# Two spellings of one filling transfer in a fused encoder layer

## The chip, the cores and the metric

The kernel runs on one core of one Trainium2 chip. The time is that of the device, in microseconds (us). The kernel before took 1100.84 us, the median of three runs (1099.44 to 1101.90).

## The reference

One layer of a streaming encoder is computed in float32 for 512 prompt rows and 64 sample rows of width 1024:

```python
h = rmsnorm(x, g_mix)
rq, rk, rv, rg, dq, dk, dv, gr, gd = project(h, w_in, pos, g_q, g_k)      # one 1024 x 8192 product
y_r = retention_out(o_r, rg, g_ret, w_ret_o)     # silu(rg) * rmsnorm(o_r), times w_ret_o
y_d = diff_out(o_d, g_sub, lam_init, w_diff_o)   # differential attention, times w_diff_o
x = x + (sigmoid(gr) * y_r + sigmoid(gd) * y_d) @ w_out
x = x + hier_moe(rmsnorm(x, g_ffn), ...)         # top-1 of 4 groups, top-2 of its 4 experts, 16 experts, SwiGLU
```

For the experts each token's row is sent to one of 640 slots of each of its two experts. The kernel fills the first 128 slots of every expert beforehand with "empty" rows (zeros, and the number of a row that no one reads).

## The kernel before

Every product with a weight is made of three matrix products on TensorE (high and low parts; lines 449 to 451). Weights come from HBM in blocks of 1 MB, `dense_load(n)`, numbered n = 0 to 43. Blocks 0 to 31 are `w_in` (16 chunks of 512 columns, two blocks each), 32 to 35 `w_diff_o`, 36 to 39 `w_ret_o`, 40 to 43 `w_out`. The block's buffer is one of four (`raw`), so that block n is issued when block n-4 has been used up. ScalarE makes the high part (`dense_hi`, line 392) and VectorE the low part (`dense_lo`, line 397), for the two blocks of the next chunk while the present chunk is multiplied, at its tiles t = 1 and t = 2. A chunk has five tiles of rows (t = 0 to 3 of the prompt, 4 of the sample), and two PSUM banks take turns: the product of a tile starts when the tile before the last one has been read out.

The order is written out by hand for each engine, and each engine works through its own list in order. SyncE (SP in the profile) issues the weight loads and the fills of the slots. GpSimd (POOL) issues everything else: it stores the projections z (`z_gr` is the last section) into HBM and loads them again as gates. Gates `gd`, `rg`, `gr` are 1280 KB halves. Each is 320 packets of 4 KB. The two halves of `rg` are issued only once all stores of z have landed (line 630 is `load_gate`). The projected gate `gd` passes a sigmoid on ScalarE (`open_gate`, line 961).

After the last chunk of `w_in` follow six chunks that are called x = 0 to 5: x = 0 and 1 multiply the attention output by `w_diff_o` (blocks 32 to 35), x = 2 and 3 the retention output by `w_ret_o`, x = 4 and 5 the merged sum by `w_out`. In x = 0 VectorE has this list for each tile: read the product out into `od` (line 1412), normalise the retention output `ro` (line 1305) and multiply it by both halves of `rg` (line 1376). In x = 1, TensorE transposes the tiles of `ro` (line 1624), ScalarE and VectorE split them (`s_hi`, line 829; `s_lo`, line 1161).

The scratch tensor `x_slots` in HBM has rows of 1056 floats (4224 bytes), 640 for each of 16 experts, and 256 rows of padding. It is filled by four transfers, one behind each of blocks 32 to 35, each for four experts (line 521), by one for the padding (line 525) and one more that sets two tiles of `y` (line 526), both behind block 36. Nothing reads them before the tokens are sent out, from 735.6 us on.

Of the kernel before, what the change touches and what calls it, by code (L numbers as in the profile page):

```python
# [14 lines left out]
P = 128  # L15
# [16 lines left out]
NE, NG, EPG = 16, 4, 4  # L32
NR = NG + NE
CAP = TT * P
XW = D_MODEL + 32
# [77 lines left out]
def build(nc, a, o):  # L113
# [161 lines left out]
    def scratch(name, rows, cols):  # L275
        return nc.dram_tensor(name, (rows, cols), f32, kind="Internal").ap()
# [5 lines left out]
    x_slots = scratch("x_slots", PAD + 2 * P, XW)  # L282
# [7 lines left out]
    def sem(name):  # L290
        return nc.alloc_semaphore(name)
# [31 lines left out]
    y_init, slots_empty = sem("y_init"), sem("slots_empty")  # L323
# [12 lines left out]
    def chunk_block(n):  # L336

        c, half = divmod(n, BPC)
        if c < IN_CHUNKS:
            w, c0 = a["w_in"][0], SECTION[c][1]  # L340
        else:
            p, j = divmod(c - IN_CHUNKS, 2)
            w, c0 = a[("w_diff_o", "w_ret_o", "w_out")[p]][0], j * COLS
        return w[half * 512:(half + 1) * 512, c0:c0 + COLS].rearrange("(k p) c -> p k c", p=P)
# [4 lines left out]
    def number(j, i, q):  # L349
        return PASS0 + PASS_BLOCKS * j + EB * i + q  # L350

    def expert_block(i, q):
        return EB * i + q - 2
# [8 lines left out]
    def dense_raw(n):  # L362
        return n % WR if n < LAST else WR + n - LAST
# [10 lines left out]
    def raw_of(i, q):  # L374
        return raw_slots[RAW_ORDER[expert_block(i, q) % RAW]]

    def full_of(i, q):
        return raw_full[RAW_ORDER[expert_block(i, q) % RAW]]
# [65 lines left out]
    def x2_done(t):  # L444
        return out_unit(5, t) + 1
# [46 lines left out]
    @block.sync  # L492
    def _(sp):
        def dense_load(n):
            if n == LAST:
                sp.wait_ge(state_stored, 32 * H)
            elif n > LAST:
                sp.wait_ge(src_ready, 3 * TT)
            elif n >= WR:
                sp.wait_ge(blocks_used, n - WR + 1)  # L500
            sp.dma_start(raw_slots[dense_raw(n)].rearrange("p (k c) -> p k c", k=4), chunk_block(n))\
                .then_inc(raw_full[dense_raw(n)], 16)

        def load_x(t):
            sp.dma_start(x_tok[:, t, :], a["x_prompt"][0, t * P:(t + 1) * P, :]).then_inc(x_in[t], 16)

        load_x(0)
        sp.dma_start(gmix[:, :], a["g_mix"][0].partition_broadcast(P)).then_inc(gmix_in, 16)
        dense_load(0)
        sp.dma_start(gen[:, :], a["c_gen"]).then_inc(gen_in, 16)  # L510
        load_x(1)
        dense_load(1)
        load_x(2)
        load_x(3)
        sp.dma_start(x_tok[0:SAMPLE, PT, :], a["x_sample"][0]).then_inc(x_in[PT], 16)
        for n in range(2, N0):
            dense_load(n)
            g = n - BPC * IN_CHUNKS
            if 0 <= g < NG:
                e = EPG * g  # L520
                sp.dma_start(x_slots[e * CAP:(e + EPG) * CAP, :].rearrange("(e c) x -> c e x", e=EPG)[0:P, :, :],
                             a["c_empty"][g % 2].unsqueeze(1).to_broadcast([P, EPG, XW])).then_inc(slots_empty, 16)
            elif g == NG:
                both = a["c_empty"].rearrange("s p x -> (s p) x")
                sp.dma_start(x_slots[PAD:PAD + 2 * P, :], both).then_inc(slots_empty, 16)
                sp.dma_start(y_dram[SINK:SINK + 2 * P, :], both[:, 0:D_MODEL]).then_inc(y_init, 16)

        def expert_load(j, i, q, e, kind, part):

            m = expert_block(i, q)  # L530
            if j is None and m < RAW:
                if m < 2:
                    sp.wait_ge(blocks_used, LAST - 2)
                elif m < WR + 2:
                    sp.wait_ge(blocks_used, LAST - 1 + m - 2)
                elif m == 6:
                    sp.wait_ge(p_evacuated, TT * OUT_CHUNKS - 1)
                elif m == 7:
                    sp.wait_ge(p_evacuated, TT * OUT_CHUNKS)
                elif m == 8:  # L540
                    sp.wait_ge(y_init, 16 * (TT + 1))
                    for k in range(2):
                        sp.wait_ge(x_loaded[k], 16)
            else:
                sp.wait_ge(blocks_used, number(0 if j is None else j, i, q) - RAW + 1)
            w, e = a[kind][0], EXPERT[e]
            if kind == "w_down":
                src = w[e, part * 256:(part + 1) * 256, :].rearrange("(p k) c -> p k c", p=P)
                dst = raw_of(i, q).rearrange("p (k c) -> p k c", k=2)
            else:  # L550
                src = w[e, part * 512:(part + 1) * 512, :].rearrange("(p k) c -> p k c", p=P)
                dst = raw_of(i, q).rearrange("p (k c) -> p k c", k=4)
            sp.dma_start(dst, src).then_inc(full_of(i, q), 16)

        def keep_x2(t):
            sp.wait_ge(p_evacuated, x2_done(t))
            sp.dma_start(y_dram[t * P:(t + 1) * P, :], x2[:, t, :]).then_inc(y_init, 16)

        def expert_pass(j):

            for i in range(NE):
                for q, (kind, part) in enumerate((("w_up", 0), ("w_up", 1), ("w_gate", 0), ("w_gate", 1))):
                    if j is None and i == 0 and q == 2:
                        for t in ORDER[:PT]:
                            keep_x2(t)
                    expert_load(j, i, q if i else 2 + q, i, kind, part)
                if j is None and i == 0:
                    keep_x2(ORDER[PT])
                for part in range(2 if i else 0):
                    expert_load(j, i, 4 + part, i - 1, "w_down", part)  # L570
            for part in range(2):
                expert_load(j, NE, part, NE - 1, "w_down", part)

        expert_pass(None)
        sp.wait_ge(npass_ready, 1)
        passes = sp.value_load(npass[0:1, 0:1], min_val=1, max_val=TT)
        with sp.If(passes > 1):
            with sp.Fori(1, passes) as j:
                expert_pass(j)
# [3 lines left out]
    def _(pool):  # L583
# [49 lines left out]
        for c, (kind, _, c0) in enumerate(SECTION[0:PURE]):  # L633
            if c == PURE - 1:
                pool.wait_ge(tr_evacuated, small_n["head", 0, HEAD_USES - 1] + 1)
                load_keys(1)
                pool.wait_ge(stage_stored[0], stored(PURE - 2, 0))
                load_values(0)
            if c in DVE_CHUNKS:
                pool.wait_ge(z_staged, DVE_CHUNKS.index(c) + 1)  # L640
            else:
                pool.wait_ge(z_evacuated, TT * (c + 1))
            if kind in "kv":
                dma(tiles(z[kind], c0, c0 + COLS, 0, PT), stage[c % 3][:, 0:PT, :]).then_inc(stage_stored[c % 3], 16)
                dma(z[kind][PROMPT:REAL, c0:c0 + COLS], stage[c % 3][0:SAMPLE, PT, :])\
                    .then_inc(stage_stored[c % 3], 16)
            else:
                dma(tiles(z[kind], c0, c0 + COLS), stage[c % 3][:, :, :]).then_inc(stage_stored[c % 3], 16)
            if c == 4:
                for s in range(3):  # L650
                    pool.wait_ge(stage_stored[s], stored(3, s))
                load_keys(0)
                for n, name in enumerate(("lambda_q1", "lambda_k1", "lambda_q2", "lambda_k2")):
                    dma(lam_in[:, n, :], a[name][0].partition_broadcast(P)).then_inc(lam_loaded, 16)
                dma(hide_in[:, :], a["c_hide"]).then_inc(lam_loaded, 16)

        for u in range(TT * PURE, TT * IN_CHUNKS):
# [30 lines left out]
            else:  # L688
# [15 lines left out]
                if r == 17:  # L704
                    pool.wait_ge(kw_ready, H)
                    pool.wait_ge(tr_evacuated, small_n["ret", H - 1, 2] + 1)
                    for k in range(TT):
                        pool.wait_ge(ring_stored[k], 16 * (14 - PURE))
                    load_gate("gd", 0, 0)
            kind, _, c0 = SECTION[c]  # L710
            pool.wait_ge(z_evacuated, u + 1)
            dma(z[kind][t * P:(t + 1) * P, c0:c0 + COLS], ring[:, t, :]).then_inc(ring_stored[t], 16)
# [428 lines left out]
    def _(dve):  # L1141
# [78 lines left out]
        def lambdas():  # L1220
# [7 lines left out]
            v.tensor_copy(hide[:, :], hide_in[:, :]).then_inc(mask_ready, 1)  # L1228

        for c, (kind, _, _) in enumerate(SECTION[0:PURE]):  # L1230
            zc = stage[c % 3][:, :, :]
            if c in DVE_CHUNKS[1:]:
# [788 lines left out]
```

## Time and profile before

| what | value |
|---|---|
| median of three runs | 1100.84 us (1099.44 to 1101.90) |
| the profiled execution | 1100.84 us, of which the span takes 1099.0 us |
| TensorE busy | 1030.2 us (94%) |
| VectorE, ScalarE, GpSimd busy | 649.1, 514.5, 154.1 us |
| moved by the 16 DMA engines | 238.38 MB |
| fill of the slots, line 521 | 4 transfers of 2112 KB, median 16.1 us from issue to landing |

The profile is of one execution. Its page gives the busy time of each engine and cuts the span into 40 slices of 27.5 us, with a digit for the busy share in tenths. The trace behind it can be asked for a stretch: which instructions ran on an engine and what ended the idle time ahead of them, the chain of waits that ended last, and how many DMA packets each queue moved. q1 (hardware_dynamic) holds what SyncE issues, q0 (software_dynamic) what GpSimd issues. Both are served by the same 16 DMA engines. In a row of issues the letter q behind an engine's name means its sequencer.

### The profile page before, as it was taken

The numbers are of one execution on the slowest core, as the hardware profiler recorded it, in microseconds if no ns is written. First come the engines' busy times: TensorE is split into PE (matmuls) and PEld (weight loads), VectorE is DVE, ScalarE is ACT, GpSimd is POOL, SyncE is SP. The second block draws the span as 40 slices with busy tenths as digits, with TensorE's granted clock in tenths as the row PEclk, the third lists the DMA queues.
The fourth block names the chain that finished last, engine by engine and source line by source line (L and its number), as shares of the span: only waits on it lengthen the run. The fifth ranks groups of instructions, "written<-read, shape, count | busy, mean of one in ns | idle before, by whom it ended". The sixth has DMA issues, their size and how long they took to land.

```text
span 1099.0 us, 12140 instructions
## 1 busy us (share of the span) xinstructions
PE 1030.2 (94%) x4736; PEld 832.0 (76%) x4736; DVE 649.1 (59%) x899; ACT 514.5 (47%) x690; POOL 154.1 (14%) x180
## 2 busy tenths in 40 slices
PE   4999999999999999999997999999299999999995
PEld 3788887887777777787785788778278888888884
DVE  4677765234444353344232845668678888989890
ACT  3533233334454343333243121254558787878771
POOL 1000020111211200211102000011102121212111
PEclk9999999999999999999999999999599999999998
DMA  9143355362624513424559644215899999999983
GB/s 304 47 144 126 125 194 177 117 236 71 211 89 152 198 62 120 144 96 144 217 181 400 244 154 154 77 78 174 321 422 363 384 406 384 406 384 406 384 328 53
DMA packets 62099, 238.38 MB, mean 217 GB/s; under 512 B 5393, under 2 KB 5569, under 8 KB 49585
## 3 DMA queue, kind: packets, MB, share of 16 engines
q1 hardware_dynamic: 41152, 163.32, 38.9%
q0 software_dynamic: 20880, 74.19, 20.3%
q8 instruction: 40, 0.66, 0.2%
q14 instruction: 27, 0.21, 0.1%
HBM read 200.12 MB, written 48.15 MB: 226 GB/s over the span
## 4 chain that ended last, share of the span: by engine, by line
PE 72%; issue 13%; DMA 5%; DVE 4%; ACT 3%; POOL 2%; SPq 0%; POOLq 0%; ACTq 0%; DVEq 0%
PE ps L449 17%; PE ps L451 17%; PE ps L450 17%; PE ps L1648 3%; PE ps L1649 3%; PE ps L1664 2%; PE ps L1701 2%; PE ps L1798 2%; PE ps L1624 2%; DMA gate<-z_rg 1%; PE ps L1730 1%; PE ps L1781 1%; DMA raw<-in_w_in 1%; DMA z_gr<-stage 1%; POOL out_y L761 1%
## 5 line engine op out<-in xcount | busy, mean ns | idle before, releaser
L449 PE MATMUL ps<-w_hi,s_hi 128*128 128x512 f32 x672 | 271.0, 403 | 9.9 <-DVE od L1412 7.1
L451 PE MATMUL ps<-w_lo,s_hi 128*128 128x512 f32 x672 | 263.7, 392 | 0.0
L450 PE MATMUL ps<-w_hi,s_lo 128*128 128x512 f32 x672 | 263.5, 392 | 0.0
L449 PEld LDWEIGHTS ps<-w_hi,s_hi 128*128 128x128 f32 x672 | 127.6, 190 | 38.4 <-issue 9.9
L451 PEld LDWEIGHTS ps<-w_lo,s_hi 128*128 128x128 f32 x672 | 127.2, 189 | 27.1
L450 PEld LDWEIGHTS ps<-w_hi,s_lo 128*128 128x128 f32 x672 | 127.5, 190 | 26.6 <-issue 1.0
L875 ACT ACTIVATE stage<-ps,x_rstd 128x512 f32<-128x512 f32 x64 | 43.9, 688 | 215.1 <-PE ps L451 215.1
L397 DVE TENSOR_TENSOR w_lo<-raw,w_hi 128x2048 fp32r<-128x2048 f32 x42 | 96.2, 2291 | 49.5 <-ACT w_hi L392 49.3
L392 ACT CAST w_hi<-raw 128x2048 fp32r<-128x2048 f32 x42 | 80.0, 1909 | 13.5 <-DMA raw<-in_w_in 8.2
L451 PE MATMUL ps<-lo_x,x_hi 128*128 128x512 f32 x192 | 75.1, 391 | 0.0
L761 POOL DMA_INDIRECT out_y<-y_exp,s_idx x15 | 43.4, 2894 | 223.2 <-ACT y_exp L1101 223.2
L421 DVE TENSOR_TENSOR lo_x<-raw_x,w_hi 128x2048 fp32r<-128x2048 f32 x32 | 71.9, 2287 | 4.4 <-ACT w_hi L410 4.3
L421 DVE TENSOR_TENSOR lo_x<-raw_x,hi_x 128x2048 fp32r<-128x2048 f32 x32 | 71.7, 2285 | 2.3 <-ACT hi_x L410 2.3
L1648 PE MATMUL ps<-w_hi,s_hi 128*128 128x512 f32 x168 | 67.6, 402 | 0.0
L1649 PE MATMUL ps<-w_lo,s_hi 128*128 128x512 f32 x168 | 66.3, 395 | 0.0
L410 ACT CAST w_hi<-raw_x 128x2048 fp32r<-128x2048 f32 x32 | 60.2, 1938 | 2.8 <-PE ps L451 2.4
L410 ACT CAST hi_x<-raw_x 128x2048 fp32r<-128x2048 f32 x32 | 59.9, 1931 | 0.1
L449 PE MATMUL ps<-w_hi,x_hi 128*128 128x512 f32 x136 | 55.2, 406 | 1.4 <-DVE x_lo L1560 1.4
L450 PE MATMUL ps<-w_hi,x_lo 128*128 128x512 f32 x136 | 54.4, 400 | 0.0
L449 PE MATMUL ps<-hi_x,x_hi 128*128 128x512 f32 x128 | 51.0, 398 | 2.0 <-issue 1.4
L829 ACT CAST s_hi<-ps 128x512 fp32r<-128x512 f32 (+1 forms) x50 | 25.2, 544 | 57.6 <-PE ps L1624 57.4
L821 ACT COPY fold<-ps 64x512 f32<-64x512 f32 x22 | 12.8, 583 | 82.3 <-PE ps L1649 82.2
(289 smaller groups left out, 1786.0 us busy)
## 6 DMA issues: line engine op xcount, KB each, us to landing
raw<-in_w_in SPq DMA_DIRECT2D x32, 1024.0 KB, 7.4
raw_x<-in_w_up SPq DMA_DIRECT2D x30, 1024.0 KB, 12.5
raw_x<-in_w_down SPq DMA_DIRECT2D x18, 1024.0 KB, 11.9
raw<-in_w_gate SPq DMA_DIRECT2D x16, 1024.0 KB, 11.3
raw_x<-in_w_gate SPq DMA_DIRECT2D x16, 1024.0 KB, 12.4
raw<-in_w_down SPq DMA_DIRECT2D x14, 1024.0 KB, 11.0
x_slots<-in_c_empty SPq DMA_DIRECT2D x4, 2112.0 KB, 16.1
x_exp<-x_slots POOLq DMA_DIRECT2D x16, 528.0 KB, 13.0
```

The source lines that it names most:

```text
L392: nc.scalar.copy(hi_slots[dense_hi_at(n)], raw_slots[dense_raw(n)]).then_inc(hi_ready, 1)
L397: nc.vector.tensor_tensor(lo_slots[dense_raw(n)], raw_slots[dense_raw(n)], hi_slots[dense_hi_at(n)].bitcast(f32), ALU.subtract).then_inc(l ...
L410: nc.scalar.copy(hi_of(i, q), raw_of(i, q)).then_inc(hi_ready, 1)
L421: nc.vector.tensor_tensor(lo_of(i, q), raw_of(i, q), hi_of(i, q).bitcast(f32), ALU.subtract).then_inc(lo_ready, 1)
L449: nc.tensor.matmul(out, s_h, w_h, start=first, stop=False)
L450: nc.tensor.matmul(out, s_l, w_h, start=False, stop=False)
L451: return nc.tensor.matmul(out, s_h, w_l, start=False, stop=last)
L761: pool.indirect_dma_start(out=y_dram, out_offset=bass.IndirectOffsetOnAxis(ap=s_idx[:, i:i + 1], axis=0), in_=y_exp[i % 2][:, :], in_offse ...
L829: nc.scalar.copy(s_hi[:, 4 * half:4 * half + 4, t * P:t * P + rows], ps[:, source_bank(u), :].rearrange("p (k c) -> p k c", k=4)[:, :, 0:r ...
L875: nc.scalar.activation(dst[:, t, :], ps[:, u % 2, :], func, scale=x_rstd[:, t:t + 1]).then_inc(z_evacuated, 1)
L1648: mm(bank, s_hi[:, k, rows], w_h, start=k == 0, stop=False)
L1649: last = mm(bank, s_hi[:, k, rows], w_l, start=False, stop=k == KC - 1)
```

## The change

The four fills of line 521 write the same bytes to the same places, but the two outer dimensions change places. Before, the outermost dimension is the 128 rows and the inner one the four experts. Now the outermost one is the four experts. The 128 rows of an expert lie one behind the other both in the source and in the scratch tensor, and the source has a stride of 0 over the experts.

```diff
             if 0 <= g < NG:
                 e = EPG * g
-                sp.dma_start(x_slots[e * CAP:(e + EPG) * CAP, :].rearrange("(e c) x -> c e x", e=EPG)[0:P, :, :],
-                             a["c_empty"][g % 2].unsqueeze(1).to_broadcast([P, EPG, XW])).then_inc(slots_empty, 16)
+                sp.dma_start(x_slots[e * CAP:(e + EPG) * CAP, :].rearrange("(e c) x -> e c x", e=EPG)[:, 0:P, :],
+                             a["c_empty"][g % 2].unsqueeze(0).to_broadcast([EPG, P, XW])).then_inc(slots_empty, 16)
```

The lists of TensorE, VectorE, ScalarE and GpSimd are the same. On SyncE, this is what stands around the four fills before (`raw` are the weight blocks' buffers, the figures are the transfer's dimensions, the last one contiguous):

```order
11 L501 DMA raw<-in_w_diff_o 128x4x512 [waits blocks_used]
12 L521 DMA x_slots<-in_c_empty 128x4x1056
13 L501 DMA raw<-in_w_diff_o 128x4x512 [waits blocks_used]
14 L521 DMA x_slots<-in_c_empty 128x4x1056
19 L501 DMA raw<-in_w_ret_o 128x4x512 [waits blocks_used]
20 L525 DMA x_slots<-in_c_empty 32x8448
21 L526 DMA out_y<-in_c_empty 256x1024
```

And now, in the same place of the same list:

```order
11 L501 DMA raw<-in_w_diff_o 128x4x512 [waits blocks_used]
12 L521 DMA x_slots<-in_c_empty 4x11x12288
13 L501 DMA raw<-in_w_diff_o 128x4x512 [waits blocks_used]
14 L521 DMA x_slots<-in_c_empty 4x11x12288
19 L501 DMA raw<-in_w_ret_o 128x4x512 [waits blocks_used]
20 L525 DMA x_slots<-in_c_empty 32x8448
21 L526 DMA out_y<-in_c_empty 256x1024
```

No instruction moved. Each fill was 512 pieces of 4224 bytes under an outermost count of 128, and is now 44 pieces of 49,152 bytes (12,288 floats) under an outermost count of 4.

## Rows read from the trace of the kernel before

**Rows 1.** The page: busy time, TensorE's slices, the fill's issues (KB each, us to landing).
```profile
PE 1030.2 (94%) x4736; PEld 832.0 (76%) x4736; DVE 649.1 (59%) x899; ACT 514.5 (47%) x690; POOL 154.1 (14%) x180
...
PE   4999999999999999999997999999299999999995
...
x_slots<-in_c_empty SPq DMA_DIRECT2D x4, 2112.0 KB, 16.1
```

**Rows 2.** Chain of waits, 530 to 680 us: start, length, what.
```profile
576.91 8.32 DMA z_gr<-stage
...
586.92 16.46 DMA gate<-z_rg
...
604.01 0.69 DVE od L1412
```

**Rows 3.** VectorE in order of time: start, length, instruction, [idle before, what ended it].
```profile
603.41 0.69 DVE L1376 TENSOR_TENSOR ro<-ro,gate 128x512 f32<-128x512 f32 x1 [4.87 <-DMA gate<-z_rg]
...
635.10 2.28 DVE L397 TENSOR_TENSOR w_lo<-raw,w_hi 128x2048 fp32r<-128x2048 f32 x1
```

**Rows 4.** TensorE in order of time, 600 to 646 us, the same columns.
```profile
604.85 0.77 PE L449 MATMUL ps<-w_hi,s_hi 128*128 128x512 f32 x1 [7.11 <-DVE od L1412]
...
640.64 1.03 PE L1624 MATMUL ps<-gen,ro 128*128 128x128 f32 x8
```

**Rows 5.** Stretches: limits, length, busy time (count) of five engines, clock, DMA share, GB/s.
```profile
600.00:610.00 10.00, 5.16 (x15) 4.16 (x16) 6.45 (x9) 0.00 (x0) 0.00 (x0) 0.66 0.71 270
618.00:621.00 3.00, 3.00 (x15) 2.49 (x14) 2.89 (x6) 1.79 (x1) 0.00 (x0) 1.00 1.05 442
573.00:604.00 31.00, 23.68 (x109) 18.45 (x107) 8.14 (x17) 12.87 (x17) 8.00 (x11) 0.97 0.99 379
```

**Rows 6.** SyncE's issues in order of time, 490 to 700 us.
```profile
535.49 0.37 SPq L501 DMA_DIRECT2D raw<-in_w_diff_o  x1
...
573.14 0.56 SPq L521 DMA_DIRECT2D x_slots<-in_c_empty  x1
...
614.19 0.37 SPq L501 DMA_DIRECT2D raw<-in_w_ret_o  x1
...
616.00 29.72 SPq L501 DMA_DIRECT2D raw<-in_w_ret_o  x3
```

**Rows 7.** GpSimd's issues in order of time, 490 to 700 us.
```profile
553.91 0.87 POOL L630 DMA_DIRECT2D gate<-z_gd  x1 [0.17 <-issue]
...
625.34 0.87 POOL L630 DMA_DIRECT2D gate<-z_gr  x1 [32.71 <-DVE ro L1376]
```

**Rows 8.** DMA queues at 539 to 541 us: packets, MB, share of 16 engines.
```profile
q1 hardware_dynamic: 193, 0.82, 103.1%
```

**Rows 9.** DMA queues at 617 to 618 us.
```profile
q1 hardware_dynamic: 201, 0.41, 105.5%
```

**Rows 10.** DMA queues at 586 to 588 us.
```profile
q0 software_dynamic: 135, 0.55, 67.2%
q1 hardware_dynamic: 136, 0.28, 35.7%
```

**Rows 11.** DMA queues at 592 to 598 us.
```profile
q1 hardware_dynamic: 313, 1.31, 53.2%
q0 software_dynamic: 313, 1.22, 49.4%
```

**Rows 12.** One issue each (blocks 33 and 37): us from issue to landing.
```profile
DMA to landing us min/median/max: 13.6/13.6/13.6
...
raw<-in_w_ret_o SPq DMA_DIRECT2D x1, 1024.0 KB, 11.6
```

**Rows 13.** ScalarE in order of time, 540 to 660 us.
```profile
554.48 1.92 ACT L392 CAST w_hi<-raw 128x2048 fp32r<-128x2048 f32 x1
...
619.21 1.91 ACT L392 CAST w_hi<-raw 128x2048 fp32r<-128x2048 f32 x1 [2.62 <-DMA raw<-in_w_ret_o]
...
629.56 1.93 ACT L392 CAST w_hi<-raw 128x2048 fp32r<-128x2048 f32 x1
```

## The prediction

> **What bounds the kernel now.** I read the page first. TensorE is busy 94% of the span, and only two places stand out in its slices: the first one and the one at 28 of 40, which is the change to the experts. [rows 1] So a delay elsewhere counts only if it makes TensorE wait, and then it counts in full, since nothing later has slack to give back. Then I read the chain of waits around the fills of line 521. It leaves TensorE there: the last store of `z_gr` lands 8.32 us after its issue, then the second half of gate `rg` takes 16.46 us. [rows 2] VectorE stood 4.87 us before it could use that half at 603.41, and behind it in VectorE's list is the read-out of a PSUM bank. [rows 3] So TensorE stood 7.11 us until 604.85, and the clock was 0.66 in the ten microseconds around, since it restarts at the lower level (1.2 of 2.4 GHz). [rows 4, 5] From 573 to 604 us the DMA engines were busy 0.99 of the time. [rows 5] This stretch is bound by DMA, and two of the four fills lie in it. [rows 6]
>
> **What the DMA rows say of packets.** While only a fill ran, 193 packets took 103.1% of 2 us on 16 engines: 0.17 us each. [rows 8] A weight packet (2 KB) takes 16 x 1.055 / 201 = 0.084 us. [rows 9] When both queues have work they alternate packet by packet, not byte by byte: 313 against 313 where both have 4 KB, and 135 against 136 where q1 has 2 KB and q0 4 KB. [rows 10, 11] A packet of q0 takes 16 x 2 x 0.672 / 135 = 0.16 us. [rows 10] How long does a 48 KB packet take? The nearest row is the stretch with the padding fill (32 pieces of 33,792 bytes): 442 GB/s at share 1.05 is 26.3 GB/s an engine. [rows 5] Such large pieces stand as single packets of full speed, so 49,152 bytes take about 1.85 us; I take 1.83.
>
> **The change, part by part.** It removes 512 small pieces a fill and adds 44 large ones. The cost on SyncE's list is nothing (0.56 us an issue now). [rows 6] What counts is which DMA engines get them. No transfer in q1 before has an outermost count below 16, so this price must be bounded from both sides. If the pieces are dealt over all 16 engines, each has 44/16 = 2.75 of them, 5.0 us, as against 32 x 0.17 = 5.4 us. If the outermost dimension is what is dealt, four engines get 11 each, 20.1 us a fill, 80.5 us for the four, and twelve get none. All else still needs all 16 engines, so the four set its pace. The order rows show an outermost count of 4, and all transfers that fill 16 engines have 32, 128 or 256 there; so I take four.
>
> The Trainium skill has a rule on this, in "DMA: Bandwidth & Descriptors", section "Why a DMA increments its semaphore by 16 and not by 1": the descriptor generator uses the largest number of engines up to 16 that divides the slowest dimension of both sides, and its table "Rules for kernel authors" warns of a small outermost dimension, a broadcast above all. By that rule k is 4 here. No run before the change shows a k below 16.
>
> Now one of the four engines, step by step. A q1 issue reaches the engines after 1.5 us, one of q0 after 3.0 us, and landing follows the last packet by 1.7 us; with these estimates the same sum for the kernel before gives block 33 at 549.2 (535.49 + 13.6 = 549.1 [rows 6, 12]), block 37 at 628.4 (616.0 + 11.6 = 627.6 [rows 6, 12]) and `rg` at 601.0, where 603.4 is read [rows 2]. I carry that 2.4 us over.
>
> 1. Fill A starts at 537: 11 x 1.83 + about 10 packets of q0 between = 22 us, to 559. Block 33 is behind it: 32 x 0.084 = 2.7 us, alternating with 25 packets of q0 (the gate `gd`, 320 packets, so 20 an engine, issued at 553.91 [rows 7]), 4 us: lands at 568.3 instead of 549.1. ScalarE wants it at 554.48 [rows 13], so stands 14 us; VectorE's list stands behind it, and TensorE loses about 7 us. This is covered: it stands from 597.7 anyway for `rg`. [rows 4]
> 2. Fill B: 20.1 + 1.6, to 588. Block 34, the last `z_gr` store and `gd`: to 595. `z_gr` lands at 591 instead of 585.2 [rows 2], so `rg` is issued at 592. Fill C: 11 x 1.99 = 22, to 617, and it lets through only 11 of the 40 packets of `rg`. The rest goes with block 35: 29 x 0.244 = 7 us, lands at 625.2. With the 2.4 us it is 627.6, against 603.4: **+24.2 us** for TensorE, in full.
> 3. Fill D runs from about 624 to 646 on the four engines, and SyncE's next issues (block 36, padding, `y`, block 37) queue behind it in q1. They go out at 614.2 and 616 + 24 = 638 and 640. [rows 6] Block 36 lands at 653.2. ScalarE stood for it already (2.62 us until 619.21 [rows 13]) and now stands until then, but the transposed tiles that it takes next come at 653 too: covered within 2 us. Then come the padding (2 x 1.25) and `y` (16 x 0.17 and more, beside q0), some 5.5 us, block 37 with 2.7, and alternating with 36 packets of two gate loads (issued at 625.3 + 24 [rows 7]), 5.8: lands at 667.3. ScalarE wants it at 629.56 + 24.2 = 653.8. [rows 13] VectorE makes the low part at 635.10 + 24.2 = 659.3 [rows 3] and would have it only at 667.3 + 1.9 + 2.3 = 671.5, then `s_lo`, 1.3: 672.8. TensorE's transposes of the next tile, at 640.64 before [rows 4], wait for that: about 672.4 against 664.9: **+7.5 us**. A further restart at the lower clock costs up to 2 us (the one at 604.85 pulled the mean of ten microseconds down to 0.66 [rows 5]); I count **+1**.
> 4. All later loads find the queues empty. The slots are not read before the tokens are sent out, long after fill D lands (648). Nothing is given back.
>
> Sum: 24.2 + 7.5 + 1 = 32.7 us on the profiled execution's 1100.84 us (span 1099.0 and 1.8 around it), which is also the median of the runs: 1133.5, said as 1134. The parts' own error: term 2 from 18 (the engine's time for 48 KB 10% less, and a shorter turn) to 30, term 3 from 0 to 14. Own range 1119 to 1147.
>
> **The rivals.**
> - *All 16 engines, not slower.* The place is the same; 2.75 large packets an engine take 5.0 us instead of 5.4. In q0 each packet would wait up to 1.83 us but only behind three of them. The stretch of 573 to 604 has the same work less 0.8 us: 1100 (1099 to 1102). For it: large pieces could be dealt one by one. Against: every transfer seen has its outermost count divisible by 16. It decides from the point where more than 12 engines have a share. Chance 0.10.
> - *Four engines, but q0 gets half the time rather than every other packet.* Then `rg` is not held: 10 us of work at half the pace, about 609 to 612 against 603.4, and block 37 still late by a few us: 1108 to 1116. Against it are the 135 and 136 packets of unequal size [rows 10]. Chance 0.12.
> - *Four engines and several large packets a turn.* Then q0 stands until q1 is empty. The four fills and blocks of 2.7 us end at about 625, `z_gr` lands only near then or in the gap before 588, and `rg` at 637: +34, with term 3: 1143 (1138 to 1155). For it: the store of `z_gr` has 4 packets an engine and took 8.32 us [rows 2]. Against: equal counts in the rows. Chance 0.16.
> - The forecast: 0.62.
>
> **How the numbers follow.** The likeliest is 1134 us. With a tenth left out above and a tenth below, where most of the first rival lies, the range is 1110 to 1148. Within 0.2% (2.2 us), which is about what a measurement can tell from no change, only the first rival falls, mostly: faster 0.03, same 0.07, slower 0.90.
>
> **What would show it.** Fills of line 521 would take 25 to 65 us from issue to landing instead of 16.1 [rows 1], with few packets of 48 KB and a DMA share that drops to about a quarter (four of 16 engines) from 600 to 615 and from 626 to 646, with the bytes a second down alike. ScalarE stands for block 33 until about 568. `rg` lands at about 627, and TensorE has one gap of some 20 us before it (not 7) and one of about 7 us near 665 to 672 that ends with `s_lo`. If the fills land within 16 us and the DMA share stays near 1, the first rival holds and my step of four engines is wrong. If they are slow and `rg` still lands before 612, it is the second.

## The result

The kernel with the new spelling takes 1143.82 us (1142.52 to 1144.76, four runs) against 1101.30 us beside it: 1.0389 times as long, 95% interval 1.0370 to 1.0406. The forecast was 1134, and the range 1110 to 1148. The profiled execution took 1145.95 us, with a span of 1144.1 us.

From the page of the kernel after, the rows that answer to [rows 1] (busy time; slices of TensorE, its clock and the DMA engines; issues of line 521):

```profile
PE 1034.6 (90%) x4736; PEld 834.9 (73%) x4736; DVE 649.0 (57%) x899; ACT 514.2 (45%) x690; POOL 154.7 (14%) x180
...
PE   4999999999999999999882399999569999999996
...
PEclk9999999999999999999987599999879999999999
DMA  9233453653350622543464163322889999999983
...
x_slots<-in_c_empty SPq DMA_DIRECT2D x4, 2112.0 KB
```

TensorE's busy time is the same to within 5 us. It stands above all in the 22nd and 23rd of the 40 slices (a 2 and a 3), and there the DMA engines show a 4 and a 1: TensorE waits for DMA while most of the DMA engines do nothing. One stretch of ten microseconds in it (limits, length, busy time of five engines, clock, DMA share, GB/s):

```profile
610.00:620.00 10.00, 0.00 (x0) 0.00 (x0) 0.00 (x0) 1.54 (x1) 0.00 (x0) 0.66 0.24 103
```

The page gives no landing time for line 521 now, where it gave 16.1 us [rows 1], so the forecast of 25 to 65 us can't be read from it. The packets themselves tell more. In the trace the large packets of the four fills run from 539 to 561, 569 to 591, 595 to 620 and 625 to 650 us (foretold ends: 559, 588, 617 and 646), and never more than four of them at a time.

TensorE's rows (start, length, instruction, [idle before, releaser]); the second one answers to [rows 4]:

```profile
576.22 3.41 PE L1798 MATMUL ps<-v_tok,sT 128*128 128x256 f32 x8 [7.32 <-DVE sT L1335]
...
648.55 0.77 PE L449 MATMUL ps<-w_hi,s_hi 128*128 128x512 f32 x1 [40.62 <-DVE od L1412]
```

The second wait is the same one as before, of 40.62 us and not 7.11. The first, of 7.32 us, is new: VectorE makes `sT` behind the low part of block 33 in its list, and stood 15.18 us for the high part of that block. VectorE's rows that answer to [rows 3] say what the long wait is for, the two halves of gate `rg`:

```profile
623.38 0.69 DVE L1376 TENSOR_TENSOR ro<-ro,gate 128x512 f32<-128x512 f32 x1 [23.59 <-DMA gate<-z_rg]
647.11 0.69 DVE L1376 TENSOR_TENSOR ro<-ro,gate 128x512 f32<-128x512 f32 x1 [23.04 <-DMA gate<-z_rg]
```

The second half comes at 647.1 where it came at 603.4. The two traces do not begin at the same point of the work: block 32 is issued at 534.88 here and at 533.66 before, 1.2 us apart. Counted from there the half is 42.5 us late, and that is the whole loss of the median (1143.82 less 1101.30 is 42.5). The two waits are 40.8 us of it (40.62 less 7.11, and 7.32); in the 42.5 us are also TensorE's restarts at the lower clock. ScalarE's rows that answer to [rows 13], with the landings of blocks 33, of gate `gd` and of blocks 35 and 36:

```profile
570.22 1.90 ACT L392 CAST w_hi<-raw 128x2048 fp32r<-128x2048 f32 x1 [14.41 <-DMA raw<-in_w_diff_o]
...
618.46 2.34 ACT L961 ACTIVATE gate<-gate 128x2560 f32<-128x2560 f32 x1 [23.65 <-DMA gate<-z_gd]
...
628.28 1.90 ACT L392 CAST w_hi<-raw 128x2048 fp32r<-128x2048 f32 x1 [5.70 <-DMA raw<-in_w_diff_o]
...
663.80 1.91 ACT L392 CAST w_hi<-raw 128x2048 fp32r<-128x2048 f32 x1 [2.62 <-DMA raw<-in_w_ret_o]
```

**Four engines.** The DMA queues from 626 to 646 us, while the last fill ran (packets, MB, share of 16 engines):

```profile
DMA packets 101, 2.18 MB, mean 109 GB/s; under 512 B 5, under 2 KB 5, under 8 KB 61
...
q1 hardware_dynamic: 51, 1.98, 22.9%
q0 software_dynamic: 50, 0.19, 2.3%
```

40 packets of 8 KB or more in 20 us, at a share of 22.9 + 2.3 = 25.2%: four of 16 engines, each with a large packet every 2.0 us. A large packet alone is 16 x 20 x 0.229 / 40 = 1.83 us. The rest of the 2.0 us is the 0.16 us of one 4 KB packet of q0 [rows 10]: one stands between two large ones, and the counts of the queues are 51 and 50 (the other 11 of q1 are the end of block 35). From 602 to 606 us the gates ran on the other twelve engines at full rate:

```profile
q0 software_dynamic: 329, 1.29, 78.7%
q1 hardware_dynamic: 8, 0.39, 22.7%
```

But a gate is whole only when its 20 packets on each of the four engines have come too. By 611 the twelve are done and have nothing to do, hence the share of 0.24 above.

SyncE's rows that answer to [rows 6]:

```profile
582.94 0.38 SPq L501 DMA_DIRECT2D raw<-in_w_diff_o  x1
...
585.16 6.37 SPq L521 DMA_DIRECT2D x_slots<-in_c_empty  x1
658.78 0.38 SPq L501 DMA_DIRECT2D raw<-in_w_ret_o  x1
```

Block 34 goes out at 582.94; before it was 572.73 (9.0 us later, counted from block 32). Block 36 goes out at 658.78, some 9 us after the last fill is over (649.5).

### The profile page after: what moved, and what is told of

It is laid out like the page before. It is cut to its first block, busy times and chain, and to the rows that moved or that the text cites. A ratio compares the mean times of both kernels' runs of the same rounds, so it can differ in the third digit from the quotient of the medians.

```text
span 1144.1 us, 12140 instructions
## 1 busy us (share of the span) xinstructions
PE 1034.6 (90%) x4736; PEld 834.9 (73%) x4736; DVE 649.0 (57%) x899; ACT 514.2 (45%) x690; POOL 154.7 (14%) x180
## 4 chain that ended last, share of the span: by engine, by line
PE 65%; issue 13%; DMA 9%; DVE 4%; ACT 3%; POOL 2%; another core or an unknown queue 2%; SPq 0%; POOLq 0%; ACTq 0%; DVEq 0%
PE ps L449 16%; PE ps L450 16%; PE ps L451 16%; PE ps L1648 3%; PE ps L1649 3%; DMA raw<-in_w_diff_o 3%; DMA gate<-z_rg 3%; PE ps L1664 2%; DMA q_tok<-z_q 2%; PE ps L1701 1%; PE ps L1798 1%; PE ps L1624 1%; PE ps L1730 1%; POOL out_y L761 1%
## 5 line engine op out<-in xcount | busy, mean ns | idle before, releaser
L449 PE MATMUL ps<-w_hi,s_hi 128*128 128x512 f32 x672 | 271.7, 404 | 42.0 <-DVE od L1412 40.6
L449 PEld LDWEIGHTS ps<-w_hi,s_hi 128*128 128x128 f32 x672 | 127.9, 190 | 70.6 <-issue 42.5
L410 ACT CAST hi_x<-raw_x 128x2048 fp32r<-128x2048 f32 x32 | 59.8, 1934 | 0.0
L829 ACT CAST s_hi<-ps 128x512 fp32r<-128x512 f32 (+1 forms) x50 | 25.2, 544 | 59.9 <-PE ps L1624 59.7
```

The lines of the kernel that those rows point to most:

```text
L410: nc.scalar.copy(hi_of(i, q), raw_of(i, q)).then_inc(hi_ready, 1)
L449: nc.tensor.matmul(out, s_h, w_h, start=first, stop=False)
L829: nc.scalar.copy(s_hi[:, 4 * half:4 * half + 4, t * P:t * P + rows], ps[:, source_bank(u), :].rearrange("p (k c) -> p k c", k=4)[:, :, 0:r ...
```

## Experiments

Call the four fills of line 521 A, B, C and D, behind blocks 32, 33, 34 and 35. All kernels differ from the kernel before only in these transfers, and where a fill is made of two transfers, in the count that GpSimd waits for ahead of the tokens. In the diffs below, three dots stand for code that is left out. The spelling of a fill is "old" (128x4x1056) or "new" (4x11x12288). Each was timed beside the kernel before.

### Number of engines and size of pieces

Sixteen engines, large pieces:

```diff
+                part = P // 16
-                sp.dma_start(x_slots[...].rearrange("(e c) x -> c e x", e=EPG)[0:P, :, :], ...)
+                sp.dma_start(x_slots[...].rearrange("(e s r) x -> s e (r x)", e=EPG, r=part)[0:16, :, :], ...)
```

> Each fill has an outermost count of 16 and large pieces (16x4x8448: 64 pieces of 33,792 bytes, four an engine). Theory (the outermost count of 4 leaves four DMA engines to do a fill, and the two queues alternate packet by packet): 16 engines share the fill, 4 x 1.25 = 5 us each as before the change, so the second half of gate rg lands at 602 to 604 us and the time is 1101 (1098 to 1104). Rival 'large packets': the 48 KB packets hold the other queue whatever the number of engines, so this is slow too, 1120 or more.

Measured: 1101.68 us, ratio 0.9999 (0.9985 to 1.0013). The page has its landing time again:

```profile
x_slots<-in_c_empty SPq DMA_DIRECT2D x4, 2112.0 KB, 15.3
```

and on VectorE the second half of `rg` is nearly as early as before (0.6 us later, counted from block 32):

```profile
604.61 0.69 DVE L1378 TENSOR_TENSOR ro<-ro,gate 128x512 f32<-128x512 f32 x1 [2.37 <-DMA gate<-z_rg]
```

In the trace up to 16 of the large pieces run at once. Pieces of 33,792 bytes cost nothing that can be seen when 16 engines share them.

Eight engines, the same pieces of 33,792 bytes:

```diff
+                for s in range(2):
+                    sp.dma_start(x_slots[...].rearrange("(e s r) x -> s e (r x)", e=EPG, r=16)
+                                 [0:8, :, s * 8 * XW:(s + 1) * 8 * XW], ...)
```

> Outermost count of 8, pieces of 33,792 bytes (each fill as two transfers 8x4x8448, in all 8 pieces an engine if eight engines share it). Theory: 8 x 1.25 = 10 us a fill on eight engines; played through the two queues, rg's second half lands at 611 to 613 instead of 603, TensorE waits 8 to 10 us more: 1111 (1106 to 1117). Rival 'any count below 16 falls to four engines or to one': 1140 or more. Rival 'large packets': as e1.

Measured: 1110.52 us, ratio 1.0079 (1.0054 to 1.0105), as the theory had it. In the trace never more than eight pieces of the fills run at once, and VectorE gets the second half of `rg` at 611.60, 9.2 us later than before when counted from block 32. With pieces of one size it is the count of engines that makes the difference between this kernel and the last one.

Four engines, small pieces:

```diff
+                for s in range(2):
+                    cols = slice(s * XW // 2, (s + 1) * XW // 2)
+                    sp.dma_start(x_slots[..., cols].rearrange("(e c) x -> e c x", e=EPG)[:, 0:P, :], ...)
```

> Outermost count of 4, but pieces of 2112 bytes (each fill as two transfers 4x128x528, 256 pieces an engine on four engines, about 21 us). Theory: the four engines need as long as with large pieces, but a packet of the other queue now waits 0.09 us and not 1.8, so the gates overtake: rg lands at about 609 to 613. Weight blocks stand behind the fills in their own queue: block 33 at 570, block 35 at 635 and block 36 at 665, so TensorE's waits move from rg to the blocks of weights, and the sum is again near 1140 (1130 to 1147). Rival 'share alone' (the size of the pieces has no part): rg lands at 640 or later as after the change, and the single gap of 40 us stays. Rival 'large packets alone': 1101.

Measured: 1143.06 us, ratio 1.037 (1.0339 to 1.040). The time is that of the new spelling, but another path makes it, and nothing here says that the two have to agree. What TensorE waited for from 540 to 760 us in this kernel (total, times, longest; "issue" says that the profile names no releaser):

```profile
PE ps L449 <- issue: 21.9, 1, 21.9
PE ps L1627 <- DVE s_lo L1164: 11.2, 3, 8.7
PE ps L1801 <- DVE sT L1338: 8.9, 1, 8.9
PE ps L449 <- DVE od L1415: 3.3, 1, 3.3
```

ScalarE in order of time, blocks 35 and 36:

```profile
638.18 1.90 ACT L392 CAST w_hi<-raw 128x2048 fp32r<-128x2048 f32 x1 [31.96 <-DMA raw<-in_w_diff_o]
669.76 1.90 ACT L392 CAST w_hi<-raw 128x2048 fp32r<-128x2048 f32 x1 [29.08 <-DMA raw<-in_w_ret_o]
```

VectorE uses the second half of `rg` at 612.21 (foretold 609 to 613), and TensorE's wait for it is 3.3 us. The weight blocks, which stand behind the fills, come at 638 and 670 (foretold 635 and 665). They stand partly in SyncE's list and not yet in the queue, as SyncE's sequencer is still issuing the fill ahead of them. Two rows of its issues (a fill's pair, and block 35):

```profile
586.07 27.18 SPq L523 DMA_DIRECT2D x_slots<-in_c_empty  x2
613.30 12.98 SPq L501 DMA_DIRECT2D raw<-in_w_diff_o  x1
```

So "share alone" falls, since `rg` is 35 us earlier than with large pieces. On four engines the size of the pieces decides who pays, the other queue (large) or the same one (small). With large pieces the number of engines decides how much: 1143.8, 1110.5 and 1101.7 us with 4, 8 and 16.

### Which of the four fills costs what

```diff
+                if g < 2:      # A and B new; in the others g >= 2, g >= 1 or g == 0
+                    (new spelling)
+                else:
+                    (old spelling)
```

> Only the first two fills (behind blocks 32 and 33) in the new spelling, the last two in the old one. Theory: block 33 still lands at 568 to 570 and TensorE loses 7 us near 570, a part of which the wait for rg covers; rg's second half lands at 610 to 613: 1109 (1104 to 1114). Rival 'the first two fills are wholly covered': 1101. Rival 'each fill costs a fourth of the whole': 1122.

> Only the last two fills (behind blocks 34 and 35) in the new spelling. Theory: block 33 lands at 549 as before the change, nothing happens near 570, but the gates meet 22 large packets on four engines: rg's second half lands at 630 to 634, TensorE waits 30 us more: 1131 (1125 to 1136). With e4's 8 us this is less than the 43 us of all four: the rest comes from block 33's delay, which moves the gates' issue behind block 34. Rival 'each fill costs a fourth': 1122. Rival 'only these two count, the first two are covered': 1144.

> Fills 2, 3 and 4 in the new spelling, only the first (behind block 32) in the old one. Theory: what the four fills cost beyond the last two comes from block 33, which stands behind fill 1. It delays the gates' issue by 10 us, so that gate gd's second half misses block 34 and meets large packets instead. With fill 1 old, block 33 lands at 549, fill 2 is drained before the gates come, and rg's second half lands at 632 to 634: 1130 (1126 to 1134), the same as with only the last two new (e5). Rival 'the four engines are busy 20 us longer for each fill': about 1139 to 1143, since three fourths of the fills are new and fill 2 stands directly ahead of block 34.

> Only the first fill in the new spelling. Theory: the whole of e4's price (1111.8, fills 1 and 2) is that of block 33 behind fill 1: 1110 (1107 to 1113), ScalarE waits 14 us for block 33 and rg's second half lands at about 610. Rival 'each of the two counts alike': 1105 to 1107.

| new fills | measured us | ratio (95%) | second half of `rg`, later than before by |
|---|---|---|---|
| A | 1110.92 | 1.0094 (1.0077 to 1.0110) | 9.7 us |
| A, B | 1111.83 | 1.0090 (1.0065 to 1.0115) | 8.6 us |
| C, D | 1129.17 | 1.0253 (1.0237 to 1.0268) | 27.7 us |
| B, C, D | 1129.11 | 1.0271 (1.0252 to 1.0290) | 27.8 us |
| A, B, C, D | 1143.82 | 1.0389 (1.0370 to 1.0406) | 42.5 us |

(The last column is VectorE's first use of that half less the issue of block 32, in one profiled execution each; before it is 603.41 - 533.66 = 69.8 us.) B costs nothing that can be seen, either beside A or beside C and D. A costs 10 us by itself (8 to 12) and 13 us beside B, C and D (1.0389 less 1.0271; 10 to 16). By the times alone these two could be the same; by the last column they are 9.7 and 14.7 us. The rivals that count every fill alike fall. With A alone, TensorE's waits from 540 to 760 us are these:

```profile
PE ps L1802 <- DVE sT L1339: 7.3, 1, 7.3
PE ps L449 <- DVE od L1416: 6.4, 1, 6.4
```

It stands for 7.3 us behind block 33 and then for 6.4 us for `rg`, which is hardly less than the 7.1 before. GpSimd's issue of the second half of `gd` shows why. With B, C and D new it is where it was before (45.7 us from block 32's issue in both):

```profile
580.41 0.87 POOL L634 DMA_DIRECT2D gate<-z_gd  x1
```

With A alone new it is 10.4 us later (56.1 us from block 32's issue at 533.68):

```profile
589.76 0.87 POOL L634 DMA_DIRECT2D gate<-z_gd  x1 [1.86 <-DVE st_out L1327]
```

While ScalarE stands for block 33 it reads out no tile of the last chunk of `w_in`, and the stores of `z_gr`, which GpSimd has to issue ahead of the gates, wait for that. In the kernel after it is the same:

```profile
573.00 0.56 POOL L712 DMA_DIRECT2D z_gr<-stage  x1 [17.02 <-ACT stage L875]
```

So the gates go out later by what block 33 cost, and their wait moves with it and covers nothing.

### The order and the place of the fills

New spelling, both blocks of a pair ahead of its two fills:

```diff
-            if 0 <= g < NG:
-                e = EPG * g
+            if g in (1, 3):
+                for f in (g - 1, g):
+                    e = EPG * f
+                    sp.dma_start(...)      # new spelling, as before
```

> New spelling; both blocks of a pair are issued ahead of the pair's two fills (32, 33, fill, fill, 34, 35, fill, fill). Theory: block 33 lands at 542, but the four engines have the same 80 us of fills, and the packets of z's stores and of the gates now stand among them: gate gd's first half lands at about 590 instead of 570, and rg still ends with the last fill at about 645: 1144 (1138 to 1152). Rival 'it was block 33 that cost the time': 1101 to 1115.

Measured: 1143.06 us, ratio 1.0383 (1.0367 to 1.0398). Block 33 is no longer late, but ScalarE now stands for the first half of `gd`, and TensorE for 17.5 us behind that and for 30.2 us for `rg`:

```profile
588.80 2.34 ACT L962 ACTIVATE gate<-gate 128x2560 f32<-128x2560 f32 x1 [19.38 <-DMA gate<-z_gd]
```

So block 33 is one way to pay and not the cause. Whoever stands in the four engines' queues pays. The time is as foretold (1144), but the end of the path is not: the last large packet is over at 636, and the second half of `rg` is used only at 643.59. From 637 to 643 us only q0 moves, at a share of 25.6%. These are the gates' packets that still stand on the four engines when the fills are through.

New spelling, fills behind blocks 26 to 29:

```diff
-            if 0 <= g < NG:
-                e = EPG * g
+            f = n - BPC * IN_CHUNKS + 6
+            if 0 <= f < NG:
+                e = EPG * f
...
```

> New spelling and the four fills behind blocks 26 to 29. Theory: no gate loads meet the fills, so the 40 us wait is gone; but blocks 27 and 29 stand behind a fill of 20 us in their own queue, and ScalarE wants them 19 us after their issue: twice about 9 us with nothing that covers them: 1110 (1100 to 1118). Rival 'four engines are slow for everything': 1130 or more. Rival 'only the gates suffer': 1092.

Measured: 1115.66 us, ratio 1.0135 (1.0120 to 1.0150). It lies in the range, 6 us above the middle. ScalarE stands for blocks 27 and 29:

```profile
452.01 1.90 ACT L392 CAST w_hi<-raw 128x2048 fp32r<-128x2048 f32 x1 [11.94 <-DMA raw<-in_w_in]
...
505.24 1.90 ACT L392 CAST w_hi<-raw 128x2048 fp32r<-128x2048 f32 x1 [20.21 <-DMA raw<-in_w_in]
```

TensorE stood 17.0 us behind these two in the stretch of 440 to 520 us, and block 32 goes out at 555.70, 22.0 us later than before; the other 5 of the 22 I did not take apart (restarts at the lower clock are among them). From there the second half of `rg` comes 10.0 us earlier than before (615.50 less 555.70 is 59.8, against 69.8), and TensorE does not stand for it at all. Together that is 12 of the 13.3 us by which this execution's span is longer.

Old spelling, the same place:

> Old spelling, but the four fills stand behind blocks 26 to 29 (about 420 to 500 us) where the DMA engines are two thirds idle. Theory: the stretch from 573 to 604 us loses 10.8 us of packets an engine, rg lands at about 594 to 596, TensorE's 7.1 us wait and the restart at the lower clock go: 1092 (1090 to 1096). Rival 'the wait is set by the last store of z and the latency of the loads, not by the queue': 1098 to 1101.

Measured: 1093.45 us, ratio 0.9934 (0.9919 to 0.9948). This version beats both kernels, by 7.3 us and 50 us. The profiled execution was the fastest of its six (1089.29). The stretch that answers to the last of [rows 5]:

```profile
573.00:604.00 31.00, 29.94 (x139) 24.47 (x139) 18.97 (x32) 12.09 (x16) 8.00 (x11) 1.00 0.73 266
```

The DMA share falls from 0.99 to 0.73, the second half of `rg` is used at 592.29, which is 9.0 us earlier (counted from block 32's issue, at 531.53), and TensorE's wait and its restart at the lower clock are gone. The rival "store and latency set it" falls.

## Why the prediction was right, and which step was mis-sized

- **The outermost count of 4 leaves four engines: right.** The share of 25.2%, and never more than four large packets at once, show it; with counts of 8 and 16 it is up to 8 and 16, and 1110.5 and 1101.7 us. This is what the Trainium skill says ("DMA: Bandwidth & Descriptors", "Why a DMA increments its semaphore by 16 and not by 1": the largest number up to 16 that divides the slowest dimension); here the trace agrees for 4, 8 and 16. The first rival (1100) is refuted.
- **The price of 1.83 us for 48 KB: right**, 1.83 from the rows above. (The row that the prediction took it from gives 49,152 bytes / 26.3 GB/s = 1.87 us, not 1.85.)
- **One packet of each queue in turn, also when one of them is 12 times larger: right** (51 and 50 packets). With small pieces `rg` is early and with large ones it is late, which refutes the second rival (1108 to 1116). The third, several large packets a turn, named 1143 and so came nearer in time, but it is refuted by the same equal counts: several large packets a turn would have left q0 with fewer.
- **Term 1, block 33 behind fill A: the landing right, "this is covered" wrong.** It landed at 570.2, or 569.0 on the clock of the trace before (foretold 568.3), and ScalarE stood 14.4 us (foretold 14). TensorE stood 7.3 us (foretold 7), and block 34 went out 9.0 us late, with the restart at the lower clock in it (a clock of 0.66 from 570 to 580 us). And the wait that I took for a cover starts from the same chain, as the kernels with A alone and with B, C, D show. Alone this is 10 us.
- **Term 2, `rg`: +24.2 foretold, +42.5 measured. This is the failed size**, and it lies outside the 18 to 30 that the prediction gave for it. My step 2 let all 20 packets an engine of `gd` pass together with block 34, ahead of fill C. But `gd` was issued 9 us late instead of 7, only 5.7 us before the first large packet of C (589.51 and 595.2), and so a part of it stood among the 11 large packets of C: it landed at 618.4 (foretold about 597). With that the second half of `rg` was not through when fill D began, and its last packets stood among D's, one for each 2.0 us, until 647. How much of this hangs on fill A is measured: with A old and B, C, D new the half comes 27.8 us late, not far from the 24.2, and with A new too it comes 42.5 us late. That it was just the 2 us between 7 and 9 that decided is argued from the count of packets and was not tried by itself.
- **Term 3, +7.5 and +1 for block 37: did not occur.** As `rg` came only with the end of fill D, block 36 was issued into an empty queue and ScalarE's wait for it is 2.62 us as before [rows 13]; for block 37 it does not wait.

The errors of terms 2 and 3 are +18.3 and -8.5 and partly cancel, which leaves the 10 us between 1134 and 1143.8. So the mechanism was right, but that the time still fell inside the range is in part luck: had term 3 come true beside the measured 42.5, the sum would have been 1152. Nor did the two gaps come as foretold (some 20 us before `rg` and 7 us near 670 that ends with `s_lo`): TensorE had one of 7.3 us near 570 that ends with `sT`, and one of 40.6.

## What to carry over

Look at the outermost count of every transfer as the compiled program has it: one that reads naturally (four experts, each one contiguous region) ran on a quarter of the DMA engines here, and the loads that needed all of them waited for that quarter, while the mean DMA share looked low. Before a delay is called covered by a later wait, check whether that wait's own start depends on what is delayed. A transfer that nobody needs for 200 us belongs where the DMA engines have room: that alone was worth 0.66% here, with the old spelling.

## What the runs showed that I had not expected

- The issue of fill D took SyncE 6.37 us instead of 0.56, and with four engines and small pieces a pair of issues took up to 27 us. In the new kernel nothing was due behind it. Both times earlier fills still stood on the four engines; whether it was room in the queue that SyncE's sequencer waited for was not tested.
- The page gives one landing time for the fills of a kernel. It is missing in all nine kernels in which a fill uses fewer than 16 engines, even where three of the four fills use 16 (A alone new), and it is there in the three where all use 16 (16.1, 15.3 and 17.3 us). That made it a quick sign here.
- The first fill costs 10 us alone, the second nothing that can be seen and the last two 28 us, though all four are the same transfer. With queues that are served packet by packet, the price of a transfer is a matter of what arrives while it runs.
